# Attention scores on two row halves of TensorE, and another share-out of the PSUM banks

## The reference, cut to what matters

```python
def _window_attention(q, k, v, q_pos, k_pos, sinks):
    s = jnp.einsum('...qhgd,...khd->...hgqk', q, k, preferred_element_type=jnp.float32) * (HEAD_DIM ** -0.5)
    ...
    s = jnp.where(valid[..., None, None, :, :], s, NEG_INF)
    sink = sinks.astype(jnp.float32).reshape(N_KV_HEADS, GQA_GROUP, 1, 1)
    m = jnp.maximum(jnp.max(s, axis=-1, keepdims=True), sink)
    p = jnp.exp(s - m)
    denom = jnp.sum(p, axis=-1, keepdims=True) + jnp.exp(sink - m)
    o = jnp.einsum('...hgqk,...khd->...qhgd', p / denom, v.astype(jnp.float32))
    return o.astype(q.dtype)
```

## Time and profile before

| | |
|---|---|
| median of 3 runs | 1840.55 us (1835.17 to 1846.29) |
| span of the profiled execution, first to last instruction | 1836.7 us |
| mean granted TensorE clock | 0.980 |
| TensorE busy | 1735.7 us, 94% |
| VectorE, ScalarE, GpSimd busy | 1267.8, 1050.5, 333.6 us |

### The profile page before, as it was taken

How to read it: one execution, slowest core, us unless ns; L and a number is a source line. 1 busy time by engine, 2 the same in 40 slices (tenths; PEclk the granted TensorE clock), 3 DMA queues, 4 the chain that set the end, 5 groups by cost and what they waited for, 6 DMA issues and landing times. The chain is left out here.

```text
span 1836.7 us, 27148 instructions
## 1 busy us (share of the span) xinstructions
PE 1735.7 (94%) x10322; PEld 1488.9 (81%) x10322; DVE 1267.8 (69%) x1656; ACT 1050.5 (57%) x1459; POOL 333.6 (18%) x336
## 2 busy tenths in 40 slices
PE   6999889999999999999999997899999999999994
PEld 3889768888888899999999986687877888788871
DVE  4524367888887634546355667789888999889966
ACT  4535345666666533435344534577787878787853
POOL 0000011111110000000001100234435443345310
PEclk9999899999999999999999998999999999999997
DMA  8554541111111853735474663889989898889867
GB/s 351 178 189 141 174 171 50 50 50 50 50 50 39 296 191 120 261 126 162 161 253 154 202 224 137 308 362 370 380 356 386 359 380 356 366 360 379 361 237 286
DMA packets 101301, 416.63 MB, mean 227 GB/s; under 512 B 16040, under 2 KB 43848, under 8 KB 87497
## 3 DMA queue, kind: packets, MB, share of 16 engines
q1 hardware_dynamic: 85488, 392.71, 57.2%
q0 software_dynamic: 10704, 17.73, 2.6%
q10 hardware_dynamic: 5016, 4.93, 0.9%
HBM read 384.06 MB, written 51.13 MB: 237 GB/s over the span
## 5 line engine op out<-in xcount | busy, mean ns | idle before, releaser
L1100 ACT ACTIVATE wup<-wraw 128x1024 fp32r<-128x1024 f32 x120 | 126.7, 1059 | 269.5 <-PE ps L1973 236.7
L1602 DVE TENSOR_TENSOR wlow<-wraw,wup 128x1024 fp32r<-128x1024 f32 x120 | 146.7, 1223 | 157.9 <-ACT wup L1100 157.5
L1753 DVE TENSOR_TENSOR wg_low<-wg,wg_up 128x2048 fp32r<-128x2048 f32 x68 | 152.9, 2288 | 28.9 <-ACT wg_up L1215 28.7
L1753 DVE TENSOR_TENSOR wu_low<-wu,wu_up 128x2048 fp32r<-128x2048 f32 x68 | 155.3, 2287 | 16.1 <-ACT wu_up L1221 15.4
L1753 DVE TENSOR_TENSOR wd_low<-wd,wd_up 128x2048 fp32r<-128x2048 f32 x66 | 148.6, 2291 | 11.9 <-ACT wd_up L1273 11.5
L1221 ACT ACTIVATE wu_up<-wu 128x2048 fp32r<-128x2048 f32 x68 | 129.9, 1913 | 26.0 <-PE ps L1973 26.0
L1215 ACT ACTIVATE wg_up<-wg 128x2048 fp32r<-128x2048 f32 x68 | 126.7, 1910 | 30.2 <-DMA wg<-w_gate 29.0
L1050 ACT ACTIVATE pp<-ps,ngm 128x256 f32<-128x256 f32 x128 | 59.5, 470 | 135.5 <-DVE skd L1487 119.8
L1973 PE MATMUL ps<-h_up,wup 128*128 128x384 f32 (+1 forms) x384 | 126.1, 328 | 3.0 <-DVE wlow L1602 3.0
L1973 PE MATMUL ps<-h_low,wup 128*128 128x384 f32 (+1 forms) x384 | 125.0, 325 | 0.0
L1973 PE MATMUL ps<-h_up,wlow 128*128 128x384 f32 (+1 forms) x384 | 125.0, 325 | 0.0
(11 more groups left out here) (391 smaller groups left out, 4829.3 us busy)
## 6 DMA issues: line engine op xcount, KB each, us to landing
wg<-w_gate SPq DMA_DIRECT2D x34, 2048.0 KB, 12.1
wu<-w_up SPq DMA_DIRECT2D x34, 2048.0 KB, 13.2
wd<-w_down SPq DMA_DIRECT2D x34, 2048.0 KB, 7.9
wraw<-w_ga SPq DMA_DIRECT2D x24, 512.0 KB, 3.8
wraw<-w_gr SPq DMA_DIRECT2D x24, 512.0 KB, 3.6
wraw<-w_at SPq DMA_DIRECT2D x24, 512.0 KB, 3.5
wraw<-w_lr SPq DMA_DIRECT2D x24, 512.0 KB, 3.5
wraw<-w_out SPq DMA_DIRECT2D x24, 512.0 KB, 3.6
```

What stands on the lines that cost most here:

```text
L1100: act.activation(wup[n % UP][:, :, :], wraw[n % RAW][:, :, :], ACT.Copy).then_inc(w_rounded, 1)
L1602: V.tensor_tensor(wlow[n % RAW][:, :, :], wraw[n % RAW][:, :, :], wup[n % UP][:, :, :].bitcast(F32), ALU.subtract).then_inc(w_split, 1)
L1753: V.tensor_tensor(low[:, k0:k1, :], whole[:, k0:k1, :], up[:, k0:k1, :].bitcast(F32), ALU.subtract).then_inc(done, 1)
```

## The change

Heads' scores are computed with the stationary operand read straight from oT and 64 rows on each half of TensorE, the two heads one behind the other behind both masks, each head into a bank of its own (3, 4 for even units, 5, 6 for odd). qst, GpSimd's copies and the semaphore u_staged are gone. For the banks: transpositions all go to bank 7 (before 5 and 6), the products with the values to bank 2 (before 7), the projections and gates to banks 0 and 1 (before 0 to 2; the three lru_x products of unit 0 stay in 0 to 2), the slab products to 7, 0, 1, 0, 1. The waits follow.

```diff
         def slab_bank(s):
-            return (s - 1) % 3 if s else 7
+            return (s - 1) % 2 if s else 7
+
+        def out_bank(i, o):
+            return o if i == 0 and o < 3 else o % 2
...
-            pool.memset(qst[:, :, :, :], 0.0).then_inc(u_staged, 1)
-            pool.wait_ge(u_staged, 1)
-            pool.sem_inc(u_out, 4)
-            for i in range(BLKS):
-                for u in range(KC):
-                    pool.wait_ge(u_out, 8 * i + u + 1)
-                    for a in range(2):
-                        half = slice(HD * a, HD * a + HD)
-                        pool.tensor_copy(qst[half, u % 4, a, :], oT[half, u, i * P:(i + 1) * P]).then_inc(u_staged, 1)
...
-                            act.activation(pp[:, s % 2, a, :], ps[:, 3 + s % 2, a * 2 * P:(a + 1) * 2 * P], ACT.Exp,
+                            act.activation(pp[:, s % 2, a, :], ps[:, 3 + 2 * (s % 2) + a, 0:2 * P], ACT.Exp,
...
-                u(V.tensor_reduce(mx[:, w, :], ps[:, 3 + w, :].rearrange("p (a k) -> p a k", a=2), AX_X, ALU.max))
+                u(V.tensor_reduce(mx[:, w, :], ps[:, 3 + 2 * w:5 + 2 * w, 0:2 * P], AX_X, ALU.max))
...
             def outs(i, s):
                 for o, part in halves_at(s):
-                    out = ps[:, o % 3, 0:GW]
+                    out = ps[:, out_bank(i, o), 0:GW]
                     if part == 0 or o >= 6:
-                        pe.wait_ge(proj_kept, number(i, o) - 2)
+                        pe.wait_ge(proj_kept, number(i, o) - 1)
...
             def slab(s):
                 if s:
-                    pe.wait_ge(proj_kept, number(0, min(s - 1, 2)) + 1)
-                ge(pe, ada_kept, PIECES + 1 + s - 2 if s >= 4 else 0)
+                    pe.wait_ge(proj_kept, number(0, min(s - 1, 1)) + 1)
+                ge(pe, ada_kept, PIECES + 1 + s - 1 if s >= 3 else 0)
...
                     if s < KC:
-                        pe.wait_ge(u_staged, 16 * i + 2 * s + 3)
                         pe.wait_ge(u_exp, 8 * i + s + 1)
+                        outs_of = [ps[:, 3 + 2 * (s % 2) + a, 0:2 * P] for a in range(2)]
                         for a in range(2):
-                            out = ps[:, 3 + s % 2, a * 2 * P:(a + 1) * 2 * P]
-                            mm(out, identb[:, :], masks[:, bass.ds(i, 1), :].rearrange("p a k -> p (a k)"), True, False)
-                            ins = mm(out, qst[:, s % 4, a, :], kT[:, s // 4, bass.ds(i * P, 2 * P)], False, True)
+                            mm(outs_of[a], identb[:, :], masks[:, bass.ds(i, 1), :].rearrange("p a k -> p (a k)"), True, False)
+                        for a in range(2):
+                            half = slice(HD * a, HD * a + HD)
+                            ins = mm(outs_of[a], oT[half, s, i * P:(i + 1) * P], kT[half, s // 4, i * P:i * P + 2 * P], False, True)
                         ins.then_inc(u_scores, 1)
...
                     if 1 <= s <= KC:
                         w = (s - 1) % 2
                         pe.wait_ge(u_norm, 8 * i + s)
-                        pe.wait_ge((u_kept, u_kept_a)[w], 4 * i + (s - 1) // 2 + 1)
+                        pe.wait_ge((u_kept_a, u_kept)[w], 4 * i + s // 2 + 1)
+                        if begin and s == 1:
+                            pe.wait_ge(ada_kept, PIECES + 2)
...
-                                ins = pe.transpose(ps[:, 5 + w, q * P:(q + 1) * P], pp[:, w, a, hf * P:(hf + 1) * P], ident[:, :])
+                                ins = pe.transpose(ps[:, 7, q * P:(q + 1) * P], pp[:, w, a, hf * P:(hf + 1) * P], ident[:, :])
...
                         if begin and s == 2:
-                            pe.wait_ge(ada_kept, PIECES + 2)
+                            pe.wait_ge(proj_kept, number(0, 2) + 1)
...
-                                ins = mm(ps[HD * a:HD * a + HD, 7, 0:P], vtok[:, i + hf, v0:v0 + HD],
+                                ins = mm(ps[HD * a:HD * a + HD, 2, 0:P], vtok[:, i + hf, v0:v0 + HD],
```

More of the change, by code:

```diff
@@ L234, in build @@
         u0 = tmp0 + 1032 + 56
-        qst = at("qst", [P, 4, 2, P], u0)
         pp = at("pp", [P, 2, 2, 2 * P], u0 + 1024)
@@ L409, in build @@
         s_dve, s_pe, s_act = sem("s_dve"), sem("s_pe"), sem("s_act")
-        u_staged, u_scores, u_negmax, u_exp = sem("u_staged"), sem("u_scores"), sem("u_negmax"), sem("u_exp")
+        u_scores, u_negmax, u_exp = sem("u_scores"), sem("u_negmax"), sem("u_exp")
         u_norm, u_turned, u_kept, u_kept_a, u_pv, u_out = sem("u_norm"), sem("u_turned"), sem("u_kept"), sem("u_kept_a"), sem("u_pv"), sem("u_out")
@@ L591, in o_store @@
             def o_store(i):
-                sp.wait_ge(u_out, 4 + KC * (i + 1))
+                sp.wait_ge(u_out, KC * (i + 1))
                 sp.wait_ge(st_o, 16 * (i + 1))
@@ L652, in _ @@
             sp.wait_ge(ada_done, PIECES + N_LATER)
-            sp.wait_ge(u_out, 4 + KC * BLKS)
+            sp.wait_ge(u_out, KC * BLKS)
             sp.wait_ge(st_mod, 32)
@@ L1013, in keep_outs @@
                     act.wait_ge(proj_done, number(i, o) + 1)
-                    src = ps[:, o % 3, 0:GW]
+                    at = out_bank(i, o)
+                    src = ps[:, at, 0:GW]
                     g = o % 3
@@ L1018, in keep_outs @@
                     elif o < 3:
-                        act.activation(xlp[:, XPAD + g * GW:], ps[:, o % 3, 0:GW - NS], ACT.Copy)
-                        act.activation(xls[:, :, XPAD:], ps[:, o % 3, GW - NS:GW].rearrange("p (b t) -> p b t", b=NB), ACT.Copy).then_inc(proj_kept, 1)
+                        act.activation(xlp[:, XPAD + g * GW:], ps[:, at, 0:GW - NS], ACT.Copy)
+                        act.activation(xls[:, :, XPAD:], ps[:, at, GW - NS:GW].rearrange("p (b t) -> p b t", b=NB), ACT.Copy).then_inc(proj_kept, 1)
                     elif o < 6:
@@ L1075, in act_round @@
                         act.wait_ge(u_pv, 8 * i + s - 1 + 1)
-                        act.activation(pT[:, 1, :, :], ps[:, 6, :].rearrange("p (k q) -> p k q", k=4), ACT.Copy).then_inc(u_kept_a, 1)
+                        act.activation(pT[:, 1, :, :], ps[:, 7, :].rearrange("p (k q) -> p k q", k=4), ACT.Copy).then_inc(u_kept_a, 1)
                     if s >= 2:
                         act.wait_ge(u_pv, 8 * i + s - 2 + 3)
-                        act.activation(oT[:, s - 2, bass.ds(i * P, P)], ps[:, 7, 0:P], ACT.Copy).then_inc(u_out, 1)
+                        act.activation(oT[:, s - 2, bass.ds(i * P, P)], ps[:, 2, 0:P], ACT.Copy).then_inc(u_out, 1)
                     if s >= KC:
@@ L1163, in _ @@
                 act_round(i)
-            act.wait_ge(u_out, 4 + KC * BLKS)
+            act.wait_ge(u_out, KC * BLKS)
             act.wait_ge(st_side, 64)
@@ L1575, in dve_round @@
                         dve.wait_ge(u_pv, 8 * i + s - 1 + 1)
-                        V.tensor_copy(pT[:, 0, :, :], ps[:, 5, :].rearrange("p (k q) -> p k q", k=4)).then_inc(u_kept, 1)
+                        V.tensor_copy(pT[:, 0, :, :], ps[:, 7, :].rearrange("p (k q) -> p k q", k=4)).then_inc(u_kept, 1)
                     if not begin and s >= KC:
@@ L2164, in _ @@
             pe.wait_ge(s_dve, 9)
+            pe.wait_ge(ld_masks, 16)
+            pe.wait_ge(v_kept, TILES)
             def pe_round(i, begin=False):
@@ L2189, in pe_round @@
                         pe.wait_ge((u_kept, u_kept_a)[w], 4 * i + (s - 2) // 2 + 2)
-                        pe.wait_ge(u_out, 8 * i + s - 2 + 4)
+                        ge(pe, u_out, 8 * i + s - 2)
                         if begin and s == 2:
-                            pe.wait_ge(ada_kept, PIECES + 2)
+                            pe.wait_ge(proj_kept, number(0, 2) + 1)
                         for a in range(2):
@@ L2209, in _ @@
             pe.wait_ge(proj_kept, N_PROJ - 3)
+            pe.wait_ge(u_out, KC * BLKS)
             for k in range(KC):
@@ L2217, in _ @@
                     ins.then_inc(h_free, 1)
-            pe.wait_ge(u_out, 4 + KC * BLKS)
+            pe.wait_ge(u_out, KC * BLKS)
             sources = ((h_up, h_low), (o_up, o_low), (ol_up, ol_low))
```

7 lines of the change are left out of this document (removed).

## The result

Median 1848.63 us (1843.23 to 1853.38, 17 runs) against 1841.73 us (1835.17 to 1847.52, 17 runs): ratio 1.0037, 95% interval 1.0026 to 1.0048. That is 6.9 us slower, 1.6 us above the predicted 1847, inside "within 0.5%". Of these 1.6 us, 1.2 are the kernel before itself: the prediction started from its median of three runs, 1840.55. The profiled execution has a span of 1845.9 us at a mean clock of 0.976.

What follows compares the result with a forecast made beforehand. TensorE was taken to set the pace in the rounds. Terms 7.6 + 2.3 - 2.7 = +7.2 us on the 1836.7 us span gave 1843.9, with 3.9 for the runs' median 1847.7, set to 1847 us; range 1829 to 1858.

Steps and rivals of the forecast that it cites:

- GpSimd's copies: Removing 128 staging copies, 57.8 us busy: gain 0; a faster VectorE might give a few tenths of a microsecond a round.
- The score block: First mask to first projection pass in each unit: 1.07 us instead of 1.10; gain 0.38 us a round, -2.7 us in seven.
- both emptyings: TensorE empties for about 0.09 us at each tile shape change, on entering and on leaving the row-half products.
- Rival A: Row halves in the score block need no emptying and hide their loads: 0.43 us per unit, -10 us, 1830 us; chance 0.20.
- The gate products: Last two steps of a round: products 8 and 11 wait for evictions, +1.08 us a round, +7.6 us in seven.
- One bank for turned weights: Each unit's transposition waits for the previous unit's eviction: cost 0 in later rounds, bounds 0 and +0.3 a round.
- Round 0: First round's own terms, from waits for xls, pT and gate evictions: together +2.3 us, bounds 0 and +4.
- xls: Round 0: first pT product waits for the eviction of unit 0's third x projection from bank 2, +1.08 us.
- VectorE's hand-over: Round 0: the scores behind the xls wait finish 0.85 us later and VectorE passes this on, +0.85 us.
- pT: Round 0: the last transposition waits for VectorE's eviction of pT behind its pp, +0.68 us.
- the gates' 0.32 instead of 0.8: Round 0: gate products wait for evictions as in later rounds, between +0.47 and +1.08 us, taken as +0.8.
- Rival C: Waits at gate products 8 and 11 mostly made good: +0.5 us a round, 0 in round 0; +0.8, about 1841 us; chance 0.15.

Runs made afterwards that it cites:

- e1: Kernel after, with gate products 8 to 11 spread over four banks (5, 6, 0, 1) instead of two; ratio to before 1.0007, round 45.44 us.
- e3: Kernel after with its banks, but scores on full 128 rows from GpSimd's zero-padded copies, both masks first; ratio to before 1.0031, round 46.77 us.
- e5: Kernel after, with both heads' operands read from rows 0 to 63, so both use one row half; 1866.93 us in one run, round 49.17 us.
- e6: Kernel before, plus one small product on 64 rows and 4 columns between each unit's two heads; 1853.84 us, ratio 1.0073, round 47.17 us.
- e2: Kernel after, with the masks of units 3 to 7 ahead of the pT products with the values; ratio to before 1.0013, round 46.03 us.
- e4: Kernel after with the edits of e1 and e2, and all three lru_x evictions of unit 0 together at step 0; 1838.5 us, ratio to before 0.9977.

## Why the prediction was right, point by point

The steps are the prediction's.

1. GpSimd's copies: gain 0 in the later rounds, as said. In round 0 the copies lengthened VectorE by 0.29 us, the "few tenths" that the text named and left out of the sum.
2. The score block: right in length (1.06 us for 1.07), in the two passes side by side and in both emptyings; the gain per round is 0.44 us (e1 against before; e3 against after says 0.43) for 0.38. The saving of 0.44 that the row halves offer is there, e5 shows it, and two emptyings (e6) and two open loads take 0.40 of it back. Rival A asked for neither and fell. The Trainium skill's up to 2x for a contraction of 64 (TensorEngine Tiling (Array Packing), Theoretical Speedup) would make 0.44 of the four passes' 0.88; the passes alone show it, the block does not.
3. The gate products: the mechanism, both places and the order of the waits were right, the size was 0.88 for 1.08 in rounds 1 to 6 and 1.00 (after against e1) from round 7. The term that was mis-sized is the way from ScalarE's eviction to the waiting product, taken as 0.14 us: here product 11 starts at 460.38, 0.06 us after gB ends at 460.32. That is some 0.09 at each of the two waits (0.38 for 0.47, then 0.52 for 0.61). The 0.14 us of the pT products behind oT was the wrong row to take it from. The expected wait rows of 0.4 and 0.5 us read smaller, one of 0.25 a round: the rest sits in the open load and inside a merged row.
4. One bank for turned weights: 0 in the later rounds, as said (e1's last unit takes 12.04 us, before 12.06).
5. Round 0: +2.6 for +2.3, but of other parts. xls +1.10 (for 1.08), VectorE's hand-over +0.88 (for 0.85) and pT +0.69 (for 0.68) held; VectorE's 0.29 and the gates' 0.32 instead of 0.8 were less; the lower clock's +1.05 was not in the sum. The total is close because these cancel, which is luck.

The rounds sum to 5.7 us for a predicted 7.2. The prediction had nothing behind them but a gain or loss passed on; there the lowered clock costs 1.3 to 1.5 us, in both profiles of the kernel after and in neither of the kernel before. Together that is 7.0 to 7.2 us, for the medians' 6.9 (their interval is 4.8 to 8.8). So the mechanism was right, but that 6.9 came out so near to the predicted 7.2 is partly luck: a gate term too large by 1.3 us in seven rounds stands against a loss behind the rounds that was not in the sum. Rival C, 1841 us, had the right direction for the size of the gate waits but not its extent. The spans of the profiles differ by 9.2 and 7.7 us, since the start varies by 2 to 3 us between profiles of one kernel, and the time behind the rounds by up to 4.

Whether the longer low clock in round 0 is caused by the change stays open. Two profiles of each kernel agree on it, but e6, with the banks, the waits and the 3.67 us wait of before, has it as well (0.50 in the first six passes), and e5, with those of after, has a clock of 0.78 from the transposition on. Only more profiles of the same kernels could tell.

## What to carry to other kernels

Using half of TensorE's rows for each of two products halves their passes, but entering and leaving that shape costs twice (0.09 + 0.11) us here: by this estimate it pays from about 0.4 us of saved passes on, so group products of one shape behind each other (e2) instead of interleaving. When banks are handed to one user, look at who follows himself most closely among those that lose them: here six short products behind each other lost 0.88 us a round, twice what the scores gained, and two banks that lie idle just then give all of it back (e1, e4). Look behind the stretch that was changed too: here 1.3 to 1.5 us went in products that the change doesn't touch, at a lower clock. A wait of TensorE counts only where nobody else is the bound: of two waits of 1 us for the same bank in round 0 neither cost anything, one of 0.7 us did.

## What the hardware showed that was not expected

- At a change of shape the next weights are not loaded under the running product: the load starts with the first product in the new shape, and the second follows 0.32 instead of 0.22 us, or 0.27 instead of 0.16, behind it.
- The passes on the two row halves run in pairs 7 ns apart, though kernel.py has the whole product of head 0 ahead of head 1's; on one half (e5) they follow each other.
- Going straight from column halves (128*64) to row halves (64*128) costs one emptying, not two.
- VectorE and GpSimd slow each other in either direction: VectorE's scaling 0.44 for 0.35 us, GpSimd's pair of copies 1.23 for 0.63 us.
- In five profiles of ten TensorE's clock fell among the gated products, 0.92 for 1.00 on the mean of the stretch shown, at the same products in the same order: 21.0 to 21.3 us for 19.7.
- TensorE's clock came back from its lower level at different places after the same 4.0 us wait: e1 and e4, neither with a gate wait, take 7.49 us (clock 0.77) and 8.33 us (0.69) from the transposition to round 1.
